# Order of the matmuls in the first two jobs of three projections: a second job that lags five tiles, against both jobs together with the low parts two tiles behind

## The reference

```
p   = (x * (1 + scale) + shift) @ w_in          # projection "in"
o   = concatenate([out_a, out_b]) @ w_out       # projection "out"
c   = rms_norm(layer_norm(...), g) @ mla_w_in   # projection "mla"
```

## Time and profile before

| | us |
|---|---|
| median of 3 runs | 1850.68 |
| lowest and highest | 1849.06, 1858.77 |
| the profiled execution | 1859.14 |
| its span | 1857.2 |
| TensorE (PE) busy in it | 1697.8 (91%) |
| VectorE (DVE) busy | 854.6 (46%) |
| ScalarE (ACT) busy | 735.9 (40%) |
| GpSimd (POOL) busy | 652.3 (35%) |

### The profile page before, as it was taken

The page is one execution under the profiler, slowest core; times in us unless marked ns, Lnnn a source line. Parts: engine busy times, 40 slices in busy tenths (PEclk is TensorE's granted clock), DMA queues, the critical chain, the costliest instruction groups (busy, mean ns, idle before and its releaser), DMA issues.

```text
span 1857.2 us, 29639 instructions
## 1 busy us (share of the span) xinstructions
PE 1697.8 (91%) x10594; PEld 1373.8 (74%) x10594; DVE 854.6 (46%) x1454; ACT 735.9 (40%) x1151; POOL 652.3 (35%) x385
## 2 busy tenths in 40 slices
PE   4998988778679999999999999899998999999997
PEld 4786667755456776887888888688886887888886
DVE  4628867655575443452212125656664452212125
ACT  1332333322344443452323235575765452323232
POOL 4345320002332112564444445233332554444441
PEclk8899989988889999999999999899999999999997
DMA  9432210001111112223333332222221323333331
GB/s 307 147 91 65 60 46 4 3 2 55 50 34 38 37 35 68 80 81 89 102 90 102 90 97 74 57 58 68 67 78 40 88 81 90 102 90 102 91 96 63
DMA packets 250857, 140.15 MB, mean 75 GB/s; under 512 B 10089, under 2 KB 242624, under 8 KB 250768
## 3 DMA queue, kind: packets, MB, share of 16 engines
q1 hardware_dynamic: 249072, 135.03, 25.2%
q0 software_dynamic: 1008, 1.66, 0.3%
q10 hardware_dynamic: 688, 2.23, 0.3%
HBM read 136.80 MB, written 2.10 MB: 75 GB/s over the span
## 4 chain that ended last, share of the span: by engine, by line
issue 49%; PE 19%; POOL 14%; DVE 9%; DVEq 3%; DMA 2%; ACT 2%; POOLq 1%; ACTq 0%; SPq 0%
POOL w_low L519 13%; PE bank L684 8%; PE bank L863 3%; DVE bank L1857 1%; PE bank L974 1%; DMA w_ada_piece<-in_w_ada 1%; DVEq L2237 1%; PE bank L740 1%; DVEq L1864 1%; DMA w_raw<-in_mlp_w 1%; DVE v_centred L1857 1%; DVE mix_out L1857 1%; PE bank L877 1%; PE bank L1079 1%; POOL w_low_z L534 0%
## 5 line engine op out<-in xcount | busy, mean ns | idle before, releaser
L519 POOL TENSOR_TENSOR w_low<-w_raw,w_high 128x1024 fp32r<-128x1024 f32 (+1 forms) x232 | 527.4, 2273 | 1077.3 <-ACT w_high L1361 1077.0
L684 PE MATMUL bank<-act_high,w_high 128*128 128x512 f32 x992 | 400.0, 403 | 7.7 <-POOL w_low L519 6.6
L684 PE MATMUL bank<-act_low,w_high 128*128 128x512 f32 x992 | 389.9, 393 | 0.0
L684 PE MATMUL bank<-act_high,w_low 128*128 128x512 f32 x992 | 389.7, 393 | 0.0
L1361 ACT ACTIVATE w_high<-w_raw 128x1024 fp32r<-128x1024 f32 (+1 forms) x232 | 225.5, 972 | 297.1 <-PE bank L684 274.9
L684 PEld LDWEIGHTS bank<-act_high,w_high 128*128 128x128 f32 x992 | 188.2, 190 | 61.6 <-POOL w_low L519 11.2
L684 PEld LDWEIGHTS bank<-act_high,w_low 128*128 128x128 f32 x992 | 187.8, 189 | 41.3
L684 PEld LDWEIGHTS bank<-act_low,w_high 128*128 128x128 f32 x992 | 188.2, 190 | 40.2 <-issue 3.0
L684 PE MATMUL bank<-hid_high,w_high 128*128 128x512 f32 x488 | 190.6, 391 | 4.0 <-DVE mix_out L2469 3.8
L684 PE MATMUL bank<-hid_low,w_high 128*128 128x512 f32 x488 | 190.0, 389 | 0.0
L684 PE MATMUL bank<-hid_high,w_low 128*128 128x512 f32 x488 | 189.9, 389 | 0.0
(11 more groups left out here) (514 smaller groups left out, 2920.2 us busy)
## 6 DMA issues: line engine op xcount, KB each, us to landing
w_raw<-in_mlp_w SPq DMA_DIRECT2D x128, 512.0 KB, 4.0
w_raw<-in_hgrn_w_in SPq DMA_DIRECT2D x32, 512.0 KB, 4.0
w_raw<-in_w_in SPq DMA_DIRECT2D x29, 512.0 KB, 4.0
w_ada_piece<-in_w_ada SPq DMA_DIRECT2D x6, 2048.0 KB, 13.4
w_raw<-in_w_out SPq DMA_DIRECT2D x8, 512.0 KB, 4.0
w_raw<-in_mla_w_o SPq DMA_DIRECT2D x8, 512.0 KB, 4.0
w_raw<-in_hgrn_w_o SPq DMA_DIRECT2D x8, 512.0 KB, 4.0
w_raw<-in_mla_w_in SPq DMA_DIRECT2D x6, 512.0 KB, 4.0
```

Of the source, the lines that this page charges most:

```text
L519: gp.tensor_tensor(WL[:, c0 % 2, 0:kt, 0:m], WR[:, c0 % 2, 0:kt, 0:m], WH[:, c0 % 2, 0:kt, 0:m].bitcast(F32), ALU.subtract).then_inc(w_lo, 1)
L684: mm = pe.matmul(bank[0:m, :], w[:, s, k, 0:m], a[:, k0 + k, :], start=(k == 0 and w is WH and a is hi), stop=(k == kt - 1 and w is WL))
```

## The change

In `two_jobs`, both jobs are now run together, tile by tile. In each step `k`, for each of the two jobs, TensorE waits for the high part of tile `k` and runs the two products with it (high and low weights), then waits for the low part of tile `k - 2` and runs the one product with it. Before, the second job ran five tiles behind the first, and each step waited for the tile's low part. The number of matmuls and their operands are the same. `part` stays in use elsewhere (L1130 and on); `two_jobs` doesn't call it any more.

```
-            LAG = 5
+            LAG = 2
 
             def two_jobs(c0, fr, use):
 
                 for k in range(KT + LAG):
-                    if k < KT:
-                        part(c0, (fr, 1), use, k, k + 1)
-                    if k >= LAG:
-                        part(c0 + 1, (fr, 2), use, k - LAG, k - LAG + 1)
-
+                    for c in (c0, c0 + 1):
+                        if k == 0:
+                            pe.wait_ge(w_lo, c + 1)
+                            pe.wait_ge(fr, c - c0 + 1)
+                        if k < KT:
+                            pe.wait_ge(act_hi, KT * USE[use] + k + 1)
+                            for w in (WH, WL):
+                                pe.matmul(PB[c % 2][:, :], w[:, c % 2, k, :], AH[:, k, :],
+                                          start=(k == 0 and w is WH), stop=False)
+                        if k >= LAG:
+                            pe.wait_ge(act_lo, KT * USE[use] + k - LAG + 1)
+                            mm = pe.matmul(PB[c % 2][:, :], WH[:, c % 2, k - LAG, :], AL[:, k - LAG, :], start=False,
+                                           stop=(k == KT + LAG - 1))
+                            if k == KT + LAG - 1:
+                                mm.then_inc(job_done, 1)
```

## The result

The changed kernel takes 1865.69 us (median of 9 runs, 1859.12 to 1871.61), the kernel before 1856.47 (9 runs, 1844.52 to 1860.70). The ratio is 1.0063 with a 95% interval of 1.0042 to 1.0084: between 8 and 16 us slower. The direction is the one forecast; the size is about twice the 6.05 us worked out, and the time lies outside the range of 1850 to 1862. The time is 9.0 us above the 1856.7 forecast. 5.8 us of that is the base, to which the loss was added: the median before had been 1850.68 in three runs and is 1856.47 in nine. The other 3.2 us are the loss itself, 9.2 us between the medians and not 6.05.

The account below looks back on a forecast made before the run. TensorE, full behind the first two pairs, was taken as the bound, so job 2's start decides. 3.0 + 0.25 + 0 + 2.8 = 6.05 us on 1850.7 gave 1856.7 us, range 1850.0 to 1862.0.

Parts of the forecast that it names:

- The chain of job 2's weights: First two pairs: job 2's weights wait for job 0's end, so job 2 starts 3.0 and 0.25 us later.
- The third pair is worth nothing: Third pair: ends near 518.8 instead of 523.0, but VectorE's sum stays at 528.56, so the 4 us gain counts 0.
- The low level directly behind the gaps: Behind the first two pairs: 7 matmuls at 1.2 GHz after each wait, 1.4 us a gap.
- rival C: All waits in the first two pairs cost 0.11 us each even when satisfied: 13 us slower, 1863.7; chance 0.12.
- rival A: Behind both gaps the clock stays up, so only the waits are paid: 3.25 us, 1853.9; chance 0.13.
- rival B: Job 2's weights are ready when the first two pairs end: 4.1 us gained, 1846.6; chance 0.09.
- the clock's term in the sum: Low-clock matmuls behind the two gaps of the first and second pair: 1.4 us each, 2.8 us in all.

Follow-up runs that it names:

- Own slots: The changed kernel with job 2's split weights of the first two projections in arrays of their own; ratio to the kernel before 0.9985.
- the kernel with the lagging second job: The changed kernel's high-parts-first order in all three pairs, but the second job starts five tiles behind the first; ratio to the kernel before 1.0021.
- filling both gaps: The changed kernel with 15 and 14 extra matmuls that nothing reads behind the first and second pair; ratio to the kernel before 0.9990.
- filling the first alone: The changed kernel with 15 extra matmuls that nothing reads behind the first pair only; ratio to the kernel before 1.0067 (6 runs).

## Why the prediction was wrong in size

**The chain of job 2's weights: right.** First pair 3.0 us later predicted, 2.45 measured, inside the bounds of 1.6 and 3.4. The start came at 50.01 instead of 49.65; 11 matmuls ran at the low level (the rows of the kernel before show 12, where the prediction's clock term counted some 13), and four long starts of the old order between 51.5 and 57.3 (0.6 us more than their neighbours in all) are gone. Second pair 0.25 predicted, 0.10 measured (0.3 between the second profiles). Gaps of 3.9 and 3.5 us predicted, 3.83 and 3.48 measured. Own slots take both away; that is shown.

**The third pair is worth nothing: right.** The pair ends near 518.7 (518.8 predicted), the sum of squares releases TensorE at 528.31.

**The low level directly behind the gaps: right in size, with luck in it.** 1.4 us each was taken. Behind the first, "v turned" is 4.1 us later, of which 2.45 is the start: 1.65. Behind the second, the layer-norm sum comes at 482.12, 53.46 us behind the pair's start where it was 51.75: 1.7, of which 0.10 is the start. But neither the fall nor its length is certain: one profile in six with a gap behind the second pair shows none, and behind the first gap 7 matmuls take 0.63 us in the changed kernel and 11 take 0.63 or more in the one with that pair alone.

**Satisfied waits, rival C: refuted.** In the first pair the starts stay 0.23 apart at full clock from 54.80 on, waits or not. **The level holds, rival A:** not so in the changed kernel, though one profile of another kernel shows it behind the second gap. **The weights ready in time, rival B:** did not happen; with own slots it came, at 1.4 instead of 3.2 us in the second pair, because TensorE waits for the last high tile (1.41 us) and then for the bank (0.71).

**The step that failed** is the clock's term in the sum, "1.4 us a gap, 2.8 in all". It counted only the matmuls directly behind the gaps and put all that comes later at nothing, since TensorE was seen full there ("a microsecond lost at the end of either pair is not made up by what follows there"). A full TensorE doesn't fix the time that its work takes: with 15.00 of 15.00 us busy it did 45 matmuls at a clock of 0.77 and 58 at 1.00. In the profiles the second pair's loss is followed by 4.4 us in the attention stage, 130 us later, where nothing was changed. The first pair's 4.1 us go the other way in the first pair of profiles: the scan starts at 261.1 in the changed kernel and at 261.5 before (262.2 and 260.9 in the second profiles), with 1.2 us less in the spatial products and 3.2 less in the mixing jobs. As the table shows, a shorter mixing comes without the change too; it is the luck of a profile, and the timed runs show no smaller loss for it.

The clock's share shows in the timed runs, each of which has its mean granted clock. Over the 21 runs of the changed kernel it is 0.9557 on the mean, with 1865.1 us; over some 110 of the kernel before, 0.9588 and 1855.0. Within the runs of one kernel, an execution with 0.001 more clock is 1.44 us shorter (a line through 270 runs of all kernels, each about its own kernel's mean). So about 0.0031 x 1440 = 4.5 of the 10.1 us go with the clock, where the prediction had 2.8, and 5.6 us don't, where it had 3.25 for the waits. This is a relation and no cause.

**What stays open.** Why the attention stage's clock falls together with the clock behind the second pair, over 120 us and several falls and rises in between that all kernels share. And the 5.6 us at equal clock against 2.45 + 0.10 us of later starts seen in the profile. Set against the kernel before in the same way, the new order in the first pair alone costs 3.5 us at equal clock, in the second 1.4, in the third -1.1; own slots come to -1.4, and 15 extra matmuls ahead of job 2 to 3.3. That is the order of the waits. But the kernel with the lagging second job comes to -2.2, though its second pair is 2 us longer, so such a figure is good to some 2 us at best, and it names no term for the rest.

## What to carry to other kernels

A lag between two jobs can be the cover for something else: before removing it, ask what is queued on the first job's end (here the slot of its weights, 4.1 us of ScalarE and GpSimd behind 4.1 us of matmuls), and give that its own storage first. A gap of some 3.5 us in TensorE's work can cost more than itself, and by chance; filling both gaps, or better removing them, was worth 9 to 10 us against the changed kernel, and filling the first alone gave back nothing in its 6 runs. And a term of 1 or 2 us at one place can't be read from the whole kernel's time when that varies by 12 us from run to run: compare stretches of several profiles, and run the kernel before against itself. A stretch has to begin at the change: one that begins 25 us ahead of it took in 2 us of the clock's own.

## What the runs showed of the hardware

The clock can fall late: in the changed kernel, behind a gap of 3.83 us, the first four matmuls went at full rate, behind 3.48 us the first five; then came 0.63 us each. Behind 4.14 us, in the kernel with the first pair alone, it was down from the first matmul on. Idle time of 1.94 us in the second pair left the clock up and 2.16 us was followed by a fall. The Trainium skill, "TensorE: Matmul & The Clock Gate", section "What's actually happening", says that the count of matmuls at the low level varies from run to run of one kernel. The two profiles of the kernel with the first gap filled agree, with 6 slow matmuls at the start of the first pair in one and 8 in the other, and go further: with the same gap of 3.5 us ahead of job 2 of the second projection, one had a fall and the other none.
